# Gate matrices by one 256-column matmul a token, and the gate groups spread over blocks 41 to 119

## What is computed

```
u = expert_u[ec]
a = gelu(einsum('cd,ced->ce', xc, u))
y = einsum('ce,ced->cd', gc * a, expert_v[ec])
```

## Time and profile before

| | |
|---|---|
| median of three runs | 1032.1 us |
| the profiled run | 1032.03 us |
| its span (first to last instruction) | 1030.0 us |
| PE busy | 1016.0 us, 99% of the span |
| DVE busy | 742.2 us, 72% |
| ACT busy | 432.2 us, 42% |
| POOL busy | 107.1 us, 10% |
| mean granted clock of TensorE | 0.998 |

### The profile page before, as it was taken

The page is one execution under the profiler, slowest core; times in us unless marked ns, Lnnn a source line. Parts: engine busy times, 40 slices in busy tenths (PEclk is TensorE's granted clock), DMA queues, the critical chain, the costliest instruction groups (busy, mean ns, idle before and its releaser), DMA issues.

```text
span 1030.0 us, 17462 instructions
## 1 busy us (share of the span) xinstructions
PE 1016.0 (99%) x6514; PEld 894.2 (87%) x6514; DVE 742.2 (72%) x1798; ACT 432.2 (42%) x763; POOL 107.1 (10%) x210
## 2 busy tenths in 40 slices
PE   9999999999999999999999999999999999999996
PEld 3478865999999999999999999988888888888885
DVE  1165543788999679999999975566666666666667
ACT  1245432233444755555555544443333334343441
POOL 1000000004000143333333300000000000000000
PEclk9999999999999999999999999999999999999999
DMA  9742200793555544444444455576555555555551
GB/s 334 308 162 105 83 21 0 223 343 122 183 182 182 179 155 136 141 144 144 143 136 138 139 164 184 185 245 214 195 193 196 190 197 188 200 188 200 187 181 42
DMA packets 48755, 176.52 MB, mean 171 GB/s; under 512 B 5136, under 2 KB 6176, under 8 KB 47520
## 3 DMA queue, kind: packets, MB, share of 16 engines
q1 hardware_dynamic: 48272, 173.82, 49.5%
q0 software_dynamic: 400, 1.58, 0.4%
HBM read 174.33 MB, written 1.05 MB: 170 GB/s over the span
## 4 chain that ended last, share of the span: by engine, by line
PE 97%; DVE 1%; DMA 1%; ACT 0%; SPq 0%; issue 0%; DVEq 0%
PE ps L464 95%; PE ps L643 1%; DMA arena<-in_w_tok 1%; DVE xs L1676 0%; DVE xs L1670 0%; DVE arena L1664 0%; DVE xs L1661 0%; PE ps L683 0%; PE ps L543 0%; PE ps L712 0%; PE ps L532 0%; ACT slab L973 0%; ACT arena L969 0%; SPq L358 0%; PE ps L847 0%
## 5 line engine op out<-in xcount | busy, mean ns | idle before, releaser
L464 PE MATMUL ps<-x1hl,hi 128*128 128x256 f32 x2216 | 377.7, 285 | 0.0
L464 PEld LDWEIGHTS ps<-x1hl,hi 128*128 128x128 f32 x2216 | 327.3, 192 | 0.0
L464 PE MATMUL ps<-hi,ahl 128*128 128x512 f32 x992 | 265.3, 389 | 0.0
L1114 ACT CAST hi<-slab 128x1024 fp32r<-128x1024 f32 x128 | 135.2, 1056 | 204.6 <-PE ps L464 204.4
L464 PEld LDWEIGHTS ps<-hi,ahl 128*128 128x128 f32 x992 | 186.2, 188 | 38.6
L464 PE MATMUL ps<-x1hl,lo 128*128 128x256 f32 x688 | 194.6, 283 | 0.0
L1626 DVE TENSOR_TENSOR lo<-slab,hi 128x1024 fp32r<-128x1024 f32 x128 | 156.0, 1219 | 0.0
L464 PE MATMUL ps<-lo,ahl 128*128 128x512 f32 x496 | 152.7, 389 | 0.0
L464 PEld LDWEIGHTS ps<-x1hl,lo 128*128 128x128 f32 x688 | 131.7, 191 | 0.0
L1405 DVE TENSOR_TENSOR lo<-slab,hi 128x1024 fp32r<-128x1024 f32 x86 | 106.1, 1233 | 16.3 <-ACT hi L1001 16.2
L464 PE MATMUL ps<-arena 128*128 128x128 f32 (+6 forms) x806 | 111.6, 293 | 1.9 <-DVE arena L1156 1.4
(11 more groups left out here) (201 smaller groups left out, 822.9 us busy)
## 6 DMA issues: line engine op xcount, KB each, us to landing
slab<-in_pv SPq DMA_DIRECT2D x128, 512.0 KB, 3.3
slab<-in_uT SPq DMA_DIRECT2D x107, 512.0 KB, 3.3
arena<-in_wq SPq DMA_DIRECT2D x32, 512.0 KB, 5.7
ahl_raw<-in_uT SPq DMA_DIRECT2D x21, 512.0 KB, 3.3
arena<-in_w_tok SPq DMA_DIRECT2D x2, 2048.0 KB, 16.7
arena<-in_w_out SPq DMA_DIRECT2D x1, 4096.0 KB, 13.3
arena<-in_w_tok SPq DMA_DIRECT2D x4, 512.0 KB, 8.3
arena<-in_w_tok SPq DMA_DIRECT2D x1, 1792.0 KB, 19.0
```

Of the source, the lines that this page charges most:

```text
L464: return nc.tensor.matmul(o, lhsT, rhs, start=start, stop=stop, skip_group_check=True)
L1114: nc.scalar.copy(hi[:, v_hi_slot(c), :], raw[:, v_slot(c), :]).then_inc(v_hi, 1)
```

## The change

- **The matmul.** The gates (the third row of the routing table) are split into a rounded part and a rest. The matrix with the gates becomes `pair`, 256 columns of fp32r: the rounded gates in the first 128, the rests in the other 128. The masks (`hot2`) are fp32r too. So a token takes one matmul of 256 columns in place of a float32 matmul of 128, and its result is two halves that have to be added.
- **The adding.** ACT's `save_low(g)` copies the first halves of the four tokens from PSUM to `low` (512 columns). DVE's `gate_group(g)` adds the second halves to them in two instructions: for the blocks below k = GROUP_AT[g] in place, for the others straight into `arena`; then a third instruction multiplies the k blocks' gates (4k columns) into `arena`. There is no filling with ones any more.
- **The one-hots.** POOL copies 16 columns (was 4), makes two masks (was two) and, new, the `pair` of tokens 2 and 3, which are four `tensor_scalar` with two operations (is_equal, mult) of 128 columns. ACT makes two masks (was one): two Abs and one Relu of 256 columns. DVE makes the `pair` of tokens 0 and 1, with one `scalar_tensor_tensor` of 256 columns each (was: one mask and four matrices).
- **The order.** The 64 groups go to blocks 41 to 119, four in each five blocks (`GROUP_AT`). `gelu(c)` writes the columns of the tokens whose gates are already in `arena` to `gel` and the others straight to `arena`: two instructions where both are there. `block_gate(c)` multiplies only the former (`gated_by(c)` columns, 4 to 256).
- **Buffers.** `UR` 6 to 5 and `GB` 4 to 3 (of two banks each); SP's loads for the v-phase start behind the last group.

```diff
-UR, UH = 6, 3
+UR, UH = 5, 3
-GB = 4
+GB = 3
+POOL_MASK, ACT_MASK = (0, 1), (2, 3)
+DVE_PAIR, POOL_PAIR = (0, 1), (2, 3)
+GROUP_AT = [N0 + g * 20 // 16 for g in range(GN)]
...
             def onehots(g):
-                nc.gpsimd.tensor_copy(n2[:, g % 2, :], slotT[:, 1, 4 * g:4 * g + 4]).then_inc(n2_ready, 1)
+                toks = range(4 * g, 4 * g + 4)
+                nc.gpsimd.tensor_copy(n2[:, g % 2, :], tbl[:, 4 * g:4 * g + 4, :].rearrange("p t a -> p (t a)")
+                                      ).then_inc(n2_ready, 1)
                 if g >= 2:
                     pool.wait_ge(pe_g, g - 1)
                 pool.wait_ge(n2_ready, g + 1)
-                for q in range(POOL_HOT):
-                    ins = nc.gpsimd.tensor_scalar(hot(g)[:, 0, q, :], iota, n2[:, g % 2, q:q + 1], None, ALU.is_equal)
-                ins.then_inc(oh2_ready, 1)
...
+                for q in POOL_MASK:
+                    ins = nc.gpsimd.tensor_scalar(hot2[:, g % 2, q, :], iota, n2[:, g % 2, 4 * q + 1:4 * q + 2], None,
+                                                  ALU.is_equal)
+                for q in POOL_PAIR:
+                    for part in range(2):
+                        ins = nc.gpsimd.tensor_scalar(pair[:, g % 2, q, part, :], iota, n2[:, g % 2, 4 * q:4 * q + 1],
+                                                      n2[:, g % 2, 4 * q + 2 + part:4 * q + 3 + part],
+                                                      ALU.is_equal, ALU.mult)
+                ins.then_inc(pool_hot, 1)
...
             def gates(g):
-                pe.wait_ge(oh_ready, g + 1)
-                pe.wait_ge(oh2_ready, g + 1)
-                pe.wait_ge(oh3_ready, g + 1)
+                pe.wait_ge(dve_hot, g + 1)
+                pe.wait_ge(act_hot, g + 1)
+                pe.wait_ge(pool_hot, g + 1)
                 if g >= GB:
                     pe.wait_ge(pre_gated, g - GB + 1)
+                banks = ps[:, gate_banks(g), :]
                 for q in range(4):
-                    last = mm(ps[:, gate_bank(g), q * P:(q + 1) * P], hot(g)[:, 0, q, :], hot(g)[:, 1, q, :],
-                              q == 0, True)
+                    last = mm(banks[:, q // 2, (q % 2) * S:(q % 2 + 1) * S], hot2[:, g % 2, q, :],
+                              pair[:, g % 2, q, :, :].rearrange("p a n -> p (a n)"), q % 2 == 0, True)
...
+            def save_low(g):
+                act.wait_ge(pe_g, g + 1)
                 if g >= 2:
+                    act.wait_ge(pre_gated, g - 1)
+                nc.scalar.copy(low[:, g % 2].rearrange("p c q -> p q c"),
+                               ps[:, gate_banks(g), :].rearrange("p b (q a c) -> p a (b q) c", q=2, a=2)[:, 0]
+                               ).then_inc(low_saved, 1)
...
             for c in range(NK):
                 gelu(c)
...
+                for g in range(GN):
+                    if GROUP_AT[g] == c + 1:
+                        save_low(g)
+                if c + UH < NK:
+                    u_split(c + UH)
+                for g in range(1, GN):
+                    if GROUP_AT[g] == c + 2:
+                        onehots(g)
...
+                for q in DVE_PAIR:
+                    ins = v.scalar_tensor_tensor(out=pair[:, g % 2, q, :, :], in0=iota.unsqueeze(1).to_broadcast([P, 2, P]),
+                                                 scalar=tbl[:, 4 * g + q, 0:1],
+                                                 in1=tbl[:, 4 * g + q, 2:4].unsqueeze(2).to_broadcast([P, 2, P]),
+                                                 op0=ALU.is_equal, op1=ALU.mult)
+                ins.then_inc(dve_hot, 1)
...
+            def gate_group(g):
+                k = GROUP_AT[g]
+                high = ps[:, gate_banks(g), :].rearrange("p b (q a c) -> p a c (b q)", q=2, a=2)[:, 1]
                 a = G[:, :, 4 * g:4 * g + 4]
+                both_low = low[:, g % 2]
+                dve.wait_ge(low_saved, g + 1)
+                did(v.tensor_tensor(both_low[:, 0:k, :], high[:, 0:k, :], both_low[:, 0:k, :], ALU.add))
+                v.tensor_tensor(a[:, k:NK, :], high[:, k:NK, :], both_low[:, k:NK, :], ALU.add)
+                settle()
+                dve.wait_ge(gelu_done, k)
+                v.tensor_tensor(a[:, 0:k, :], both_low[:, 0:k, :], a[:, 0:k, :], ALU.mult).then_inc(pre_gated, 1)
...
-            for c in range(N0 + GN - 2, NK):
+            for c in range(N0, NK + 1):
                 if filled[0] < NK:
                     fill()
-                block_gate(c, GN)
-                if c >= NK - 3 and c < NK - 1:
-                    a_split(c - NK + 3)
-                    v_rest(c - NK + 3)
+                for g in range(1, GN):
+                    if GROUP_AT[g] == c + 1:
+                        onehots(g)
+                for g in range(GN):
+                    if GROUP_AT[g] == c:
+                        gate_group(g)
+                if c > N0:
+                    block_gate(c - 1)
+                if NK - 2 <= c < NK:
+                    a_split(c - NK + 2)
+                    v_rest(c - NK + 2)
```

More of the change, by code:

```diff
@@ L214, in peer_layer_kernel @@
         qT = gel[:, 0, :].rearrange("p (b t) -> p b t", b=2)
-        subk_sb = small(2 * P).rearrange("p (a n) -> p a n", a=2)
+        subk_sb = slab[:, 8320 - 2 * P:8320].rearrange("p (a n) -> p a n", a=2)
+        low = slab[:, 6144 + P:6144 + P + 8 * P].rearrange("p (b q c) -> p b c q", b=2, q=4)
         dup = ahl_raw[:, 0:768]
@@ L394, in _ @@
             sp.wait_ge(x1_ready, 2)
-            for c in (0, 1, 4, 5):
+            for c in (0, 1, 4):
                 load_u(c)
@@ L1088, in save_routes, with onehots @@
                     act.wait_ge(pe_rT, t + 1)
[L1089 removed]
+                    nc.scalar.copy(tbl[:, t * P:(t + 1) * P, 0:3].rearrange("p t a -> p a t"),
                                    ps[:, 2 + t, 0:3 * P].rearrange("p (a n) -> p a n", a=3)).then_inc(rT_saved, 1)
[L1092 to L1106 removed]
+            def onehots(g):
+                if g == 0:
+                    act.wait_ge(rT_saved, T)
+                for n, q in enumerate(ACT_MASK):
+                    if n == 0 and g >= 2:
+                        act.wait_ge(pe_g, g - 1)
+                    nc.scalar.activation(hot2[:, g % 2, q, :], iota, ACT.Abs, scale=-1.0, bias=tbl[:, 4 * g + q, 1:2]
+                                         ).then_inc(hot_dist, 1)
+                act.wait_ge(hot_dist, len(ACT_MASK) * (g + 1))
+                both = hot2[:, g % 2, ACT_MASK[0]:ACT_MASK[-1] + 1, :]
+                nc.scalar.activation(both, both.bitcast(F32), ACT.Relu, scale=-1.0, bias=1.0).then_inc(act_hot, 1)
+            def save_low(g):
+                act.wait_ge(pe_g, g + 1)
+                if g >= 2:
+                    act.wait_ge(pre_gated, g - 1)
+                nc.scalar.copy(low[:, g % 2].rearrange("p c q -> p q c"),
+                               ps[:, gate_banks(g), :].rearrange("p b (q a c) -> p a (b q) c", q=2, a=2)[:, 0]
+                               ).then_inc(low_saved, 1)
             def v_split(c):
@@ L1611, in _, with block_gate @@
+            def block_gate(c):
+                n = gated_by(c)
+                dve.wait_ge(gelu_done, c + 1)
+                dve.wait_ge(pre_gated, n // 4)
+                a = arena[:, c * S:c * S + n]
+                v.tensor_tensor(a, gel[:, c % 2, 0:n], a, ALU.mult).then_inc(gated, 1)
             assert filled[0] == NROUTE
@@ L1613, in _ @@
                 fill()
-            dve.wait_ge(rT_saved, T)
+            tables()
             onehots(0)
             fill()
-            for g in range(GN):
-                fill()
-                if g + 1 < GN:
-                    onehots(g + 1)
-                gate_group(g, max(0, g - 2))
-                if g >= 2:
-                    block_gate(N0 + g - 2, g + 1)
+            fill()
+            assert filled[0] == N0 + 1
             def v_rest(c):
```

124 lines of the change are left out of this document (38 added, 86 removed).

## The result

The changed kernel takes 1153.5 us (median of four runs, 1149.1 to 1156.9) against 1032.1: a ratio of 1.117, 95% interval 1.113 to 1.122. The profiled run took 1149.1 us, 117.1 more than that of before. The forecast was 1080 us, with 1135 as the upper end: the sign and the place were right, but the loss forecast (48 us) was less than half of the measured one.

The account below looks back on a forecast made before the run. PE bounds the kernel before; after the change POOL sets the pace P, 5.3 us a group. The difference, 61 P - 275, gives +48 us, 1080 us; range 1050 to 1135, widened below to 1040.

Parts of the forecast that it names:

- PE's gain: PE's gate groups: four matmuls cost 0.48 us in place of 0.887, saving 0.407 us 64 times, 26.0 us.
- ACT: ACT's load in the gate stretch: 3.5 us a group against 4.08 allowed, fitting though narrowly within one block.
- DVE: DVE's load in the gate stretch: 3.7 us a group against 4.08, with additions priced at 1.04 ns a column.
- POOL's own work: POOL's copy and six `tensor_scalar` a group: 3.77 us undisturbed, 3.93 with 0.62 for each two-operation instruction.
- The holds: POOL stands still while DVE runs an instruction with two SBUF inputs, bringing a group to 5.3 us.
- The hand-drawn group: One group laid out at k = 80: 4.66 us, the next 5.6, two around a groupless block 10.9; 5.3 a group.
- the second rival: POOL waits through DVE's whole row of adjacent instructions, or holds DVE in turn: P = 6.8, 1172 us; chance 0.07.
- The start: Start of the gate groups: group 2 is ready at 371.15, where PE alone would ask for it at 371.92.
- The table's steps: The table's two small DVE steps lie beside PE's work, before block 41, and cost nothing.
- The clock: PE's clock falls because PE idles; gate stretch at 1.2 GHz, 8.2 us a group, +225 us; chance 0.02.
- Rival 1: PE stays the bound, POOL held less: P 4.08 to 4.3, put at 1009 us; chance 0.08.
- The second form of rival 2: POOL gets in between DVE's instructions but holds DVE for its full time; both times add, 6.8 us a group.

Follow-up runs that it names:

- The best version: Changed kernel with new layout of `low`, three pairs on DVE, one on ACT, POOL only masks, ACT's copy in write order, one-hots before `u_split`: 1014.8 us, ratio 0.983.
- the run without POOL: Changed kernel, but POOL makes its one-hots for groups 0 and 1 only and all later groups reuse them: 1021.5 us.
- the layout alone: Changed kernel with only `low` stored so that a block's four tokens lie next to each other, not 128 columns apart: 1150.1 us.
- four pairs on DVE: Changed kernel with DVE making all four pairs, POOL only two masks: 1064.5 us; with the new layout of `low` as well, 1032.5 us.

## Why the prediction was wrong, by its steps

**PE's gain: right.** 0.48 us for the four matmuls was confirmed, and with it the 26 us that PE alone would save. The best version gets 17.7 of them.

**ACT: right**, fitting and narrow (203.1 us for 61 groups, 3.3 each, forecast 3.5); it decided once its copy became longer.

**DVE: mis-sized too, without effect here.** The additions were priced at 1.04 ns a column, from the earlier trace rows, because the old multiply also had four-column steps in one operand. None of those rows reads an operand in steps of 128 columns in SBUF. In the run without POOL the three instructions cost 1.6 to 2.1 ns a column (0.66 forecast for 476 columns, 1.01 to 1.03 measured), some 0.7 us a group more. In the changed kernel this cost nothing, as the layout alone shows. With four pairs on DVE it cost 32 us (1064.5 against 1032.5); with three no run has the new layout alone.

**POOL's own work: mis-sized, the step that failed.** The forecast was 0.29 + 6 x 0.58, raised to 3.93 us; measured 4.66, which is 61 x 0.73 = 44.5 us of the 69 missing. An instruction with two operations takes 0.787 us (0.785 start to start), above the upper bound of 0.75 and far above the 0.62 taken: 0.66 us a group; the wait behind the copy adds 0.07. The upper bound was drawn without a row.

By the Trainium skill (GPSIMD Engine Reference, Elementwise — side-by-side cycle accounting) up to two operations an element cost no more than one. The measurement decides against that here: 598 ns with one and 787 with two in this kernel, and 602 for the same pairs with one.

**The holds: right in kind, 0.2 to 0.3 us short.** The forecast was 5.3 - 3.93 = 1.37 us a group, measured 1.6 to 1.7. The hand-drawn group held only what starts in a two-input instruction, as the trace does, but let POOL in at the end of each; in a quarter of the cases it waited through more than one. How much of the 0.2 to 0.3 us this makes isn't shown. That was the second rival, given 0.07 as a world of its own (P = 6.8), where it was a part of the likeliest one.

**The start: left out.** Group 2 was forecast at 371.15 and came at 379.62. POOL may only begin when DVE has split the gates. DVE does so behind a fill; that fill, then POOL's timeline:

```profile
357.50 1.23 DVE L1415 TENSOR_TENSOR hi<-slab,hi 128x1024 fp32r<-128x1024 f32 x1 [4.35 <-ACT hi L1005]
...
359.79 0.20 POOL L440 COPY n<-slab 128x16 f32<-128x16 f32 x1 [355.18 <-DVE slab L1592]
360.09 3.34 POOL L446 TENSOR_SCALAR hot<-slab,n 128x128 fp32r<-128x128 f32 x2
363.43 4.35 POOL L450 TENSOR_SCALAR pair<-slab,n 128x128 fp32r<-128x128 f32 x4
```

POOL begins 4.4 us later than in the kernel before (355.37), and then takes 7.9 us for the first group, so that even group 0 kept PE waiting for 2.3 us. The table's steps were called free. They take only 1.1 us, but they stand behind a fill that waited 4.35 us for ACT, and the engine that they delay was the bound.

**The sum**, in its own form, from 48.3 us forecast to 117.0 measured: P adds 61 x (6.26 - 5.3) = 58.6 (44.5 by POOL's own work, 14 by the holds), the start 8.5, and the last group's block at the lower clock 1.6 (27.95 us to the v-phase in place of 26.4).

**The clock: half right.** It did fall (0.02 had been given to that), and it cost next to nothing, since the 8.2 us a group priced there need a clock that stays low; it was low in pieces only, and PE had time to spare.

**Rival 1** was rightly held unlikely. The second form of rival 2, that POOL holds DVE for its whole time, didn't come: beside POOL's masks `block_gate` takes 0.07 us more, and a fill's median is 1.22 us here and 1.23 in the run without POOL. The Trainium skill (SBUF — State Buffer, Who interferes with whom) lets whoever issues first block the other for the whole instruction, and says so of those modes of DVE that take both port pairs. The trace agrees for a POOL instruction that starts in DVE's fill, and not for the other direction, where DVE loses under 0.1 us.

## What to carry to other kernels

An engine that looks idle may be idle in just the gaps that suit it: before work goes there, look which of its instructions took longer than their kin, and what ran beside them. A kind of instruction or an access pattern that no row shows needs a bound with a wide upper end, above all on the engine that the forecast itself names as the bound. And with four engines near full, a change pays only when each one's load is measured and moved in turn: the same idea that cost 12% gave 1.7% after the layout, the copy's order and the division were put right.

## What the hardware showed unexpectedly

- An instruction of POOL that starts while DVE reads two operands from SBUF is held (1.16 us a group for the fills alone); with one of the two in PSUM it isn't, and one that started 0.09 us or more ahead of DVE's isn't either. Between adjacent ones POOL gets in at the first end only in part of the cases (108 of 146); memsets of one column between them gave 14 to 18 us back.
- A `tensor_scalar` of 128 columns on POOL takes 0.60 us with one operation and 0.79 with two.
- Stepping through SBUF by 128 columns costs DVE 1.6 to 2.1 ns a column in place of 1.04. Writing every fourth column costs ACT's copy of 512 columns 1.11 us in place of 0.59, while reading PSUM in steps costs it nothing.
